# Recurrence gates of a hybrid decoder as three rounded matmuls: the convolution result and the gate weights split on ScalarE and VectorE

## The reference

```python
def layer(x, st_h, st_conv, st_gla, reset_first, p):
    h = rmsnorm(x, p['norm_pre'][0])
    x = x + 0.5 * rmsnorm(swiglu(h, ...), p['norm_post'][0])
    h = rmsnorm(x, p['norm_pre'][1])
    m, h_last, new_conv, S_fin = mixer(h, st_h, st_conv, st_gla, reset_first, p)
    x = x + rmsnorm(m, p['norm_post'][1])
    ...
```

```python
xc, new_conv = causal_conv(xl, st_conv, p['conv_w'], p['conv_b'])
r = sigmoid(einsum('btnd,nde->btne', xb, wa) + ba)
i = sigmoid(einsum('btnd,nde->btne', xb, wx) + bx)
log_a = -8 * r * softplus(-lam)
h_t = a_t * h_(t-1) + sqrt(1 - a_t^2) * i_t * xc_t
```

## Time and profile before

| | |
|---|---|
| median of 3 runs | 2164.38 us (2164.17 to 2164.51) |
| the profiled execution | 2164.07 us |
| its span, first to last instruction | 2162.0 us |
| TensorE busy | 2153.9 us, 100% |
| VectorE, ScalarE, GpSimd busy | 1440.5, 1292.4, 707.1 us |
| transfers | 350.70 MB, 162 GB/s |

### The profile page before, as it was taken

One profiled execution on the slowest core, in us unless ns is written; L12 is line 12 of the kernel. 1 busy time (PEld: TensorE's weight loads), 2 busy tenths in 40 slices (PEclk: granted clock), 3 DMA queues, 4 the chain that ended last, 5 costly groups with the idle time before them and its releaser, 6 DMA issues.

```text
span 2162.0 us, 40931 instructions
## 1 busy us (share of the span) xinstructions
PE 2153.9 (100%) x17069; PEld 2129.7 (99%) x17069; DVE 1440.5 (67%) x1898; ACT 1292.4 (60%) x1990; POOL 707.1 (33%) x708
## 2 busy tenths in 40 slices
PE   9999999999999999999999999999999999999999
PEld 9999999999999999999999999999999999999998
DVE  7555857678986658845584558577699867576454
ACT  8534657648785656653564356576577765575434
POOL 3112512525554225511240124124275533152111
PEclk9999999999999999999999999999999999999999
DMA  7555554445554465555555555554465544655553
GB/s 249 166 166 160 167 173 154 147 143 171 166 156 137 148 180 162 166 166 165 163 163 163 167 166 165 167 158 145 140 183 156 156 138 150 182 162 163 162 169 126
DMA packets 102534, 350.70 MB, mean 162 GB/s; under 512 B 11408, under 2 KB 16528, under 8 KB 102352
## 3 DMA queue, kind: packets, MB, share of 16 engines
q1 hardware_dynamic: 101664, 347.42, 52.6%
q10 hardware_dynamic: 688, 0.68, 0.1%
HBM read 343.19 MB, written 4.87 MB: 161 GB/s over the span
## 4 chain that ended last, share of the span: by engine, by line
PE 96%; DVE 1%; POOL 1%; issue 1%; DMA 0%; ACT 0%; SPq 0%; DVEq 0%; POOLq 0%; ACTq 0%
PE psD L512 91%; PE psM L605 1%; POOL ssum L1644 1%; PE psM L512 0%; DVE val L1501 0%; PE psM L647 0%; PE psM L719 0%; DVE wl L1175 0%; DMA raw<-in_w_gu 0%; PE psM L682 0%; PE psM L724 0%; POOL hidl L1845 0%; PE psS L532 0%; PE psM L734 0%; PE psD L498 0%
## 5 line engine op out<-in xcount | busy, mean ns | idle before, releaser
L512 PE MATMUL psD<-hh,wh 128*128 128x288 f32 x3664 | 1093.0, 298 | 0.6 <-DVE hl L1243 0.6
L512 PE MATMUL psD<-hl,wh 128*128 128x288 f32 x3664 | 1081.6, 295 | 0.0
L512 PE MATMUL psD<-hh,wl 128*128 128x288 f32 x3664 | 1078.3, 294 | 0.0
L1175 DVE TENSOR_TENSOR wl<-raw,wh 128x1024 fp32r<-128x1024 f32 (+2 forms) x656 | 823.6, 1256 | 112.6 <-ACT wh L828 112.1
L828 ACT ACTIVATE wh<-raw 128x1024 fp32r<-128x1024 f32 (+2 forms) x656 | 672.0, 1027 | 95.5 <-DMA raw<-in_w_gu 46.5
L512 PEld LDWEIGHTS psD<-hh,wh 128*128 128x128 f32 x3664 | 686.9, 187 | 6.3 <-issue 3.4
L512 PEld LDWEIGHTS psD<-hh,wl 128*128 128x128 f32 x3664 | 690.2, 188 | 0.0
L512 PEld LDWEIGHTS psD<-hl,wh 128*128 128x128 f32 x3664 | 688.0, 188 | 1.5
L1845 POOL TENSOR_TENSOR hidl<-hid,hidh 128x288 fp32r<-128x288 f32 x176 | 214.1, 1216 | 906.9 <-ACT hidh L1119 906.9
L512 PE MATMUL psD<-hidh,wh 128*128 128x288 f32 x1408 | 417.6, 297 | 0.4 <-POOL hidl L1845 0.4
L512 PE MATMUL psD<-hidl,wh 128*128 128x288 f32 x1408 | 415.8, 295 | 0.0
(11 more groups left out here) (258 smaller groups left out, 1586.2 us busy)
## 6 DMA issues: line engine op xcount, KB each, us to landing
raw<-in_w_gu SPq DMA_DIRECT2D x351, 512.0 KB, 3.5
raw<-in_w_d SPq DMA_DIRECT2D x128, 448.0 KB, 3.2
raw<-in_w_in SPq DMA_DIRECT2D x80, 512.0 KB, 3.5
raw<-in_w_d SPq DMA_DIRECT2D x64, 512.0 KB, 3.5
raw<-in_w_out SPq DMA_DIRECT2D x32, 512.0 KB, 3.6
x<-in_xT SPq DMA_DIRECT2D x8, 288.0 KB, 6.9
gates<-in_w_ax SPq DMA_DIRECT2D x4, 512.0 KB, 4.7
S<-in_st_gla SPq DMA_DIRECT2D x4, 512.0 KB, 4.4
```

The lines of the kernel that those rows point to most:

```text
L512: mm = e.matmul(out, w[:, kt * P:(kt + 1) * P], t[:, kt, :], start=(kt == 0 and part == 0), stop=(kt == KT - 1 and part == 2))
L1175: e.tensor_tensor(wl[u % RING][:, part], raw[u % RING][:, part], wh[u % RING][:, part].bitcast(F32), ALU.subtract).then_inc(lo_ready, 1)
```

## The change

The gates are formed like the dense units. ScalarE rounds the gate weights of a mixer to `gates_hi` in slot 2 and each tile's convolution result to `xch` in slot 4t+3. VectorE subtracts to `gates_lo` (over the memory of `gates`) in slot 3 and to `xcl` in slot 4t+3. TensorE forms each gate by three rounded matmuls and waits for `xcl_ready` instead of `xc_ready`. `xch` and `xcl` have one buffer each, which lies over `bc`, so the first write of `bc` in slot 18 waits for the last gates; `gates_hi` lies over `qf`.

```diff
+    bc_at = cursor[0]
     bc = sb("bc", [P, PR, T])
...
+    qf_at = cursor[0]
     qf = sb("qf", [P, PR, NSL - 2, C])
+    end_at = cursor[0]
+    cursor[0] = bc_at
+    xch, xcl = (sb(k, [P, T], F32R) for k in ("xch", "xcl"))
+    cursor[0] = qf_at
+    gates_hi = sb("gates_hi", [P, LT, 2 * P], F32R)
...
+    cursor[0] = hid_at
+    gates_lo = sb("gates_lo", [P, LT, 2 * P], F32R)
...
     # TensorE, recurrence
-                    e.wait_ge(xc_ready, q + 1)
+                    e.wait_ge(xcl_ready, q + 1)
                     if q:
                         e.wait_ge(i_ready, q)
                     if t == 0:
-                        e.wait_ge(gates_landed, 16 * (i + 1))
+                        e.wait_ge(gates_split, i + 1)
...
                     for gate_of in (0, 1):
-                        mm = e.matmul(psM[:, gate_of, 0:T], gates[:, t, gate_of * P:(gate_of + 1) * P], tile_of(xc[g], t)[:, :], start=True, stop=True)
+                        own = slice(gate_of * P, (gate_of + 1) * P)
+                        e.matmul(psM[:, gate_of, 0:T], gates_hi[:, t, own], xch[:, :], start=True, stop=False)
+                        e.matmul(psM[:, gate_of, 0:T], gates_hi[:, t, own], xcl[:, :], start=False, stop=False)
+                        mm = e.matmul(psM[:, gate_of, 0:T], gates_lo[:, t, own], xch[:, :], start=False, stop=True)
                     mm.then_inc(gates_done, 1)
...
     # ScalarE, recurrence
+                if slot == 2:
+                    e.wait_ge(gates_landed, 16 * (i + 1))
+                    if i:
+                        e.wait_ge(wide_done, 3 * i)
+                    e.activation(gates_hi[:, :, :], gates[:, :, :], ACT.Copy).then_inc(gates_rounded, 1)
+                if slot % R_PERIOD == 3 and t < LT:
+                    q = LT * i + t
+                    e.wait_ge(xc_ready, q + 1)
+                    if q:
+                        e.wait_ge(gates_done, q)
+                    e.activation(xch[:, :], tile_of(xc[g], t)[:, :], ACT.Copy).then_inc(xch_ready, 1)
...
     # VectorE, recurrence
+                if slot == 3:
+                    e.wait_ge(gates_rounded, i + 1)
+                    e.tensor_tensor(gates_lo[:, :, :], gates[:, :, :], gates_hi[:, :, :].bitcast(F32), ALU.subtract).then_inc(gates_split, 1)
+                if slot % R_PERIOD == 3 and t < LT:
+                    e.wait_ge(xch_ready, q + 1)
+                    if q:
+                        e.wait_ge(gates_done, q)
+                    e.tensor_tensor(xcl[:, :], tile_of(xc[g], t)[:, :], xch[:, :].bitcast(F32), ALU.subtract).then_inc(xcl_ready, 1)
...
                 if slot == 18:
                     steps.after(sub)
+                    e.wait_ge(gates_done, LT * i + LT)
```

More of the change, by code:

```diff
@@ L249, in program @@
     cv_end = cursor[0]
+    qf_at = cursor[0]
     qf = sb("qf", [P, PR, NSL - 2, C])
+    end_at = cursor[0]
[3 more added lines that the diff above has]
+    gates_hi = sb("gates_hi", [P, LT, 2 * P], F32R)
+    assert cursor[0] <= end_at
     cursor[0] = qkv_at
@@ L347, in program @@
     tap_ready = sem("tap_ready")
+    gates_rounded, gates_split, xch_ready, xcl_ready = (sem(k) for k in ("gates_rounded", "gates_split", "xch_ready", "xcl_ready"))
     ident_landed = sem("ident_landed")
```

## The result

The changed kernel takes 2174.27 us (2174.06 to 2174.55) beside 2164.45 us (2164.17 to 2164.57) for the kernel before: 9.8 us more, a ratio of 1.0046 with an interval of 1.0034 to 1.0058. The forecast was 2171.0 with a range to 2175.5. The sign and the place were right, and 3.3 us of the size were missing. The profiled execution spans 2172.2 us where the one before spanned 2162.0: +10.2 to account for.

The account below looks back on a forecast made before the run. TensorE, busy 2153.9 of 2162.0 us, was taken as the bound; mixer nets of 3.85, 3.75, -0.35 and -0.35 summed to +6.9 us on 2164.07, giving 2171.0 us, with a range from 2167.0 to 2175.5.

Parts of the forecast that it names:

- TensorE's own part: All 16 gate groups: six rounded matmuls take 0.80 us in place of 0.97, a gain of 2.7 us in all.
- the other end (1.45): Gate groups, bound from the other side: rounded matmuls at 0.24 us each make a group 1.45, losing 7.7 us.
- First tile: Tile 0 of each mixer: TensorE waits 0.33 us in the first mixer, not at all in the second.
- the release: Time from a VectorE end to the matmul that waited for it: 0.14 us read, 0.15 added.
- Tiles 1 and 2: Second and fourth mixer: TensorE newly waits for the subtraction, 2.0 us at tile 1 and about 2.5 at tile 2.
- rival 1: Mixers 2 and 4: only one wait each, 2.0 us at tile 1, nothing more at tile 2; 2166.0 us; 15%.
- Tile 3: Second mixer: the low part is ready at 607.51, TensorE comes at 608.2; no wait, 0.7 us to spare.
- Waits taken at their length: Mixers 2 and 4: each wait counted at its length alone, 4.2 us late by tile 2, 3.85 net in the second.
- rival 4: Four waits cost more than their length through a clock drop or restarts, 2 us each, 2179 us; 6%.
- rival 3: Tile 1 or 2 of mixers 2 and 4: subtraction blocked by GpSimd's pair addition, up to 2.46 us; 2175 us; 12%.
- ScalarE is not what is late: Tile 1 of the second mixer: ScalarE's place for the rounding is in front of the logits at 573.30.
- It decides at the place of L1243 and at stretched rows before it: Mixers 2 and 4: VectorE reaching its subtraction 1.5 us earlier would hide everything, 2162.0 us; 5%.

Follow-up runs that it names:

- experiment 4: The changed kernel without VectorE's subtraction for tile 1 in mixers 2 and 4 (`xch` stands in for `xcl` there): 2174.10 us, ratio 1.0042.
- experiment 8: The changed kernel with VectorE's recurrence issued first in each slot, ahead of the other group's normalisation with its operand split: 2174.25 us, ratio 1.0046.
- Experiment 1: The changed kernel without VectorE's subtraction of any tile; TensorE uses `xch` in place of `xcl`, with as many matmuls: 2166.47 us, ratio 1.0008.
- 7: The changed kernel with TensorE's gate groups one unit later and VectorE's subtraction of tiles 1 to 3 one slot earlier: 2166.94 us, ratio 1.0011.
- experiment 5: The changed kernel with VectorE's subtraction of tiles 1 to 3 one slot earlier (4t+2), nothing else moved: 2171.04 us, ratio 1.0030.
- experiment 3: The changed kernel without the subtraction for tiles 2 and 3 in mixers 2 and 4 (`xch` in place of `xcl` there): 2167.85 us, ratio 1.0016.

## Why the prediction was right, and what its sum missed

**TensorE's own part: right in kind, 0.3 us too large.** Six matmuls take 0.80 us as forecast in the first mixer's tiles 1 to 3, but from group to group the gain is 0.153 and not 0.17, so 2.45 in all where 2.72 was forecast. The 0.97 of the plain group was read at its edge, from one pair of starts. A group near the other end (1.45) came only in the fourth mixer's tile 2, 1.35 long, with the clock falling in it.

**First tile: right in place, 0.33 forecast, 0.21 measured.** The term that was off is the release. I took 0.15 from a VectorE end to its waiting matmul; here it is 0.06 (314.83 + 0.45 = 315.28, L617 at 315.34; 593.75 + 0.44 = 594.19, L617 at 594.25). Six times 0.09 is most of the difference between the 9.7 us of waiting in the forecast and the 8.95 found.

**Tiles 1 and 2: right.** The forecast put `xcl` 577.93 - 562.05 = 15.88 us and 594.02 - 562.05 = 31.97 us after the mixer's first gates; it started 15.86 and 31.94 after them. The waits are 1.89 and 2.39 for 2.0 and 2.5. That VectorE does not catch up while TensorE stands was the reason for the second wait against rival 1, and experiment 4 shows it from the other side.

**Tile 3: right, no wait, but the working was off.** The forecast let VectorE's backlog last and put `xcl` 606.90 - 562.05 = 44.85 us after the first gates; it started 608.60 - 561.81 = 46.79 after them. VectorE had caught up behind tile 2 (idle for 1.83 us before 600.07, for a unit's result), so it came late with TensorE. About 0.4 us were to spare for the 0.7 forecast, in a mixer that the clock had delayed; in the second mixer of experiment 8, at full clock, tile 3 lost 0.02. Experiment 1 adds that ScalarE would hold it by 0.48 if TensorE came earlier.

**Waits taken at their length: the step that failed.** The sum put waits at their length and left the clock and the restarts to rival 4, with 6%. Both happened: 2 x 1.52 for the clock and 6 x 0.10 for restarts, 3.6 us. With 0.3 less gain at the gates and 0.7 less waiting, that makes 3.2 of the 3.3 us between the forecast +6.9 and the +10.2 of the spans. The range held because it had been drawn up to 2175.5 for another reason, the lock of rival 3, which did not come. Rival 4 overshot (2179) because it gave four waits 2 us each, and only two brought a fall, of 1.5 us. Falls came in four traces, all with waits of 2.4 us or more, and in none whose longest wait in the mixers was 1.9; no row of the kernel before could tell that.

**"ScalarE is not what is late": true at tile 1, wrong at tile 2.** I read its place before tile 1 alone. It changed nothing in the sum, since the subtraction was later still, but the expectations of experiments 1 and 7 missed by it, and that of 5 in part.

**"It decides at the place of L1243 and at stretched rows before it": half right.** Experiment 8 took the first away and the wait stayed, by the second, a stretched weight split. The condition there was also misread: VectorE would have had to be 2.0 us earlier, not 1.5, since what must be in time is the subtraction's end, and 2.5 earlier at tile 2. Rival 3 was right as a mechanism (1.70 us, experiment 5) and did not meet the change's own places.

## What to carry to other kernels

When an operand of a saturated engine gets one more producer, work out the time at which the last producer's queue reaches it, tile by tile, from the trace: here that gave the four large waits to about 0.1 us. Then compare remedies by what they move: a consumer issued one unit later gave back 9.7 us, while reordering the late engine's queue or starting its work earlier passed the backlog to the next item that it owed. And before counting on the gain of such a remedy, look for the second-latest producer, which the first hides.

## What was not expected of the hardware

- The clock can fall in or after a wait of a few microseconds and stays down for a while though TensorE is busy again: 3.4 us each time, once 6.8. The falls began between 1.1 us before and 1.1 us after TensorE's restart. It fell after 2.39 and 2.37 (the change), 3.97 and 3.91 (experiment 4) and 3.14 (5), not after 1.9, nor after 2.51 in experiment 5; and of two waits of 2.83 and 2.84 in one execution (8) it fell after one. So the wait's length alone does not decide in this range; what does, these runs leave open.
- The first rounded matmul after a wait takes 0.10 us longer to the next start, also at full clock, and also after a wait of 0.02 us (608.64 in experiment 8).
- The start of the kernel moves between programs that are the same there: the first gates come between 315.13 (the change) and 316.58 (experiment 3) where they came at 315.09, mostly in TensorE's wait for `hl` within the first 11 us. I did not find the cause; up to 1.5 us of a difference between two of these kernels can be this and nothing else.
